# One decoder block on one core: the last column block of the output product and the layer norm behind it, rearranged

## What is computed

```
u   = x * (1 + scale) + shift
q, k, v, z_a, B, C, xc, z_b, g_a, g_b = split(u @ W_in)
...                                    # differential attention -> yA, short convolution -> yB
h   = sigmoid(g_a) * (yA @ P_a) + sigmoid(g_b) * (yB @ P_b)
out = h @ W_out
r   = 2**0.25 * x + gate * out
y   = (r - mean(r)) * rsqrt(var(r) + 1e-5) * ln_gain + ln_bias      # over the 2048 columns
```

## Time and profile before

| what | us |
|---|---|
| median of 3 runs | 1530.58 (1530.0 to 1531.59) |
| the profiled execution, its own time | 1531.4 |
| its span, first to last instruction | 1529.7 |
| PE busy in the span | 1478.7 (97%) |
| DVE busy | 860.4 (56%) |
| ACT busy | 515.6 (34%) |
| POOL busy | 67.6 (4%) |

### The profile page before, as it was taken

The page is one execution under the profiler, slowest core; times in us unless marked ns, Lnnn a source line. Parts: engine busy times, 40 slices in busy tenths (PEclk is TensorE's granted clock), DMA queues, the critical chain, the costliest instruction groups (busy, mean ns, idle before and its releaser), DMA issues.

```text
span 1529.7 us, 18414 instructions
## 1 busy us (share of the span) xinstructions
PE 1478.7 (97%) x6624; PEld 1211.3 (79%) x6624; DVE 860.4 (56%) x1182; ACT 515.6 (34%) x725; POOL 67.6 (4%) x99
## 2 busy tenths in 40 slices
PE   4999989999999999999999999999999999999993
PEld 3888867878878788887888878887888888888882
DVE  6978667658475574656756568333432323533447
ACT  2333553253432534425344253232122121411121
POOL 0000000000000000000000000100000000000004
PEclk9999999999999999999999999999999999999997
DMA  9979525352453524444254442632323232363212
GB/s 354 385 261 381 172 69 159 97 154 80 142 158 114 154 80 141 142 130 137 82 157 124 142 127 81 224 109 83 109 84 108 84 110 82 111 247 110 82 55 110
DMA packets 212359, 219.18 MB, mean 143 GB/s; under 512 B 8418, under 2 KB 160738, under 8 KB 211554
## 3 DMA queue, kind: packets, MB, share of 16 engines
q1 hardware_dynamic: 201264, 176.52, 35.3%
q0 software_dynamic: 10096, 35.66, 7.8%
q10 hardware_dynamic: 962, 6.53, 1.1%
HBM read 211.33 MB, written 7.34 MB: 143 GB/s over the span
## 4 chain that ended last, share of the span: by engine, by line
PE 95%; DVE 3%; DMA 1%; ACT 1%; issue 0%; SPq 0%; POOLq 0%; POOL 0%; ACTq 0%; DVEq 0%
PE acc L1251 29%; PE acc L1253 29%; PE acc L1252 29%; PE sc L1350 1%; PE misc L1373 1%; PE sc L1251 1%; PE sc L1253 1%; PE sc L1252 1%; DMA w_mod_in<-in_w_mod 1%; PE sc L1364 1%; DVE res L1234 1%; DVE res L1210 0%; PE sc L1300 0%; PE misc L1300 0%; PE misc L1356 0%
## 5 line engine op out<-in xcount | busy, mean ns | idle before, releaser
L1251 PE MATMUL acc<-act_hi,w_hi 128*128 128x512 f32 x1472 | 578.9, 393 | 9.9 <-ACT q_raw L503 6.1
L1253 PE MATMUL acc<-act_hi,w_lo 128*128 128x512 f32 x1472 | 574.6, 390 | 0.0
L1252 PE MATMUL acc<-act_lo,w_hi 128*128 128x512 f32 x1472 | 574.4, 390 | 0.0
L503 ACT ACTIVATE w_hi<-raw 128x1024 fp32r<-128x1024 f32 (+1 forms) x258 | 269.9, 1053 | 773.6 <-PE acc L1253 619.5
L774 DVE TENSOR_TENSOR w_lo<-raw,w_hi 128x1024 fp32r<-128x1024 f32 (+1 forms) x258 | 311.0, 1213 | 388.6 <-ACT w_hi L503 388.6
L1251 PEld LDWEIGHTS acc<-act_hi,w_hi 128*128 128x128 f32 x1472 | 277.4, 188 | 71.5 <-ACT q_raw L503 6.6
L1253 PEld LDWEIGHTS acc<-act_hi,w_lo 128*128 128x128 f32 x1472 | 277.2, 188 | 58.5
L1252 PEld LDWEIGHTS acc<-act_lo,w_hi 128*128 128x128 f32 x1472 | 277.5, 189 | 57.0 <-issue 0.2
L984 DVE SCALAR_TENSOR_TENSOR bias_acc<-bias_w,mod,bias_acc 128x512 f32<-128x512 f32 x48 | 36.1, 751 | 124.7 <-DMA bias_w<-in_w_in 124.7
L1253 PE MATMUL acc<-y_hi,w_lo 128*128 128x512 f32 x256 | 100.3, 392 | 0.0
L1252 PE MATMUL acc<-y_lo,w_hi 128*128 128x512 f32 x256 | 100.3, 392 | 0.0
(11 more groups left out here) (170 smaller groups left out, 1058.5 us busy)
## 6 DMA issues: line engine op xcount, KB each, us to landing
raw<-in_w_in SPq DMA_DIRECT2D x256, 256.0 KB
raw<-in_w_tail SPq DMA_DIRECT2D x32, 1024.0 KB
raw<-in_w_in SPq DMA_DIRECT2D x25, 1024.0 KB
w_mod_in<-in_w_mod SPq DMA_DIRECT2D x32, 512.0 KB, 8.6
w_mod_in<-in_w_mod SPq DMA_DIRECT2D x16, 1024.0 KB, 9.2
gate_in<-in_w_mod POOLq DMA_DIRECT2D x32, 512.0 KB, 4.3
bias_w<-in_w_in POOLq DMA_DIRECT2D x48, 256.0 KB, 3.3
x_in<-in_xT SPq DMA_DIRECT2D x8, 512.0 KB, 8.4
```

What stands on the lines that cost most here:

```text
L503: return act.activation(dst, src, ACT.Copy)
L1251: pe.matmul(dst, a_hi, b_hi, start=first, stop=False)
L1252: pe.matmul(dst, a_hi, b_lo, start=False, stop=False)
L1253: return pe.matmul(dst, a_lo, b_hi, start=False, stop=last)
```

## The change

In the last column block only two halves are shared by all token tiles (`SHARED` = 2). The other six are kept: four in the slots, and two in buffers of their own, `w_end_hi` and `w_end_lo`, which lie where part of `x_tok` lay. Each token tile then goes through six halves. Accordingly ACT and DVE handle halves 3, 4 and 5 of the block by the old rule and halves 6 and 7 without waiting for a slot.

The norm is made by DVE for all 2048 columns of every tile, in two instructions of 1024 columns, in the last tile in three of 1024, 640 and 384 (`Y_PARTS`). ACT makes only the square root, POOL has no part in it, `shift_col` is gone, and SP issues all stores, one for each part.

x is loaded into `res` itself, once all of h is split (`h_split` in place of `h_ready`); the product with `gate` goes into a new tile, `gated`, and L1210 reads `res` and `gated` and writes `res`.

```diff
--- before.py
+++ after.py
@@ -19,6 +19,8 @@
 
 
 from contextlib import ExitStack
+
+import itertools
 
 import numpy as np
 
@@ -57,8 +59,9 @@
 SHIFT_SLOTS = 4
 SHIFTS = D // COLS
 SCALE_STEPS = GROUPS * MOD_CHUNKS * MOD_STEPS
-V_COLS = (896, 896, 1024, 1600)
-V_FIRST = tuple(c * 5 // 8 for c in V_COLS)
+Y_PARTS = (((0, 1024), (1024, 2048)),) * (NT - 1) + (((0, 1024), (1024, 1664), (1664, 2048)),)
+Y_COUNT = tuple(itertools.accumulate(len(parts) for parts in Y_PARTS))
+SHARED = 2
 LEAD = 3
 SLOTS = 4
 
@@ -143,7 +146,7 @@
         stats = sb("stats", [P, NT, D // COLS, 6])
         mean_var = sb("mean_var", [P, NT, 2])
         rstd = sb("rstd", [P, NT])
-        shift_col = sb("shift_col", [P, NT])
+        sb("to_grid", [P, 4])
 
         raw = sb("raw", [P, 2, 4, COLS])
         w_hi = sb("w_hi", [P, SLOTS, 2, COLS], F32R)
@@ -194,7 +197,9 @@
         z_b, e_b, o_sq, rms = q_raw, q_rot, k_raw, k_rot
         h, y_hi, y_lo = stage([("h", [P, KT, T], F32), ("y_hi", [P, HEADS, T], F32R),
                                ("y_lo", [P, HEADS, T], F32R)])
-        res, x_tok = stage([("res", [P, NT, D], F32), ("x_tok", [P, NT, D], F32)])
+        res, w_end_hi, w_end_lo, gated = stage([
+            ("res", [P, NT, D], F32), ("w_end_hi", [P, 2, 2, COLS], F32R), ("w_end_lo", [P, 2, 2, COLS], F32R),
+            ("gated", [P, NT, COLS], F32)])
 
         acc = ctx.enter_context(nc.psum_tensor("acc", [P, 4, COLS], F32))
         sc = ctx.enter_context(nc.psum_tensor("sc", [P, 3, 512], F32))
@@ -282,10 +287,6 @@
         step = sem("step")
         var_ready = sem("var_ready")
         std_ready = sem("std_ready")
-        norm_ready = sem("norm_ready")
-        normed = sem("normed")
-        pool_step = sem("pool_step")
-        pool_ready = sem("pool_ready")
         y_ready = sem("y_ready")
         stored = sem("stored")
 
@@ -336,13 +337,6 @@
                 pool.wait_ge(g_stored[n], 16)
             for e in range(ENDS):
                 pool.dma_start(h[:, 4 * e:4 * e + 4, :], g_raw[:, 4 * e:4 * e + 4, :]).then_inc(g_back[e], 16)
-
-            for t in range(NT):
-                tail = res[:, t, V_COLS[t]:D]
-                pool.wait_ge(normed, t + 1)
-                pool.tensor_tensor(tail, tail, ln_g[:, V_COLS[t]:D], ALU.mult).then_inc(pool_step, 1)
-                pool.wait_ge(pool_step, t + 1)
-                pool.tensor_tensor(tail, tail, ln_b[:, V_COLS[t]:D], ALU.add).then_inc(pool_ready, 1)
 
 
         @block.sync
@@ -486,15 +480,10 @@
                 for s in range(4):
                     plain_unit(w_tail, s, i * COLS, i, 4, O0 // 2 + s)
             for t in range(NT):
-                for n in range(2):
-                    cols = slice(n * V_FIRST[t], V_COLS[t] if n else V_FIRST[t])
-                    sp.wait_ge(y_ready, 2 * t + n + 1)
-                    sp.dma_start(out[t * P:(t + 1) * P, cols], res[:, t, cols]).then_inc(stored, 16)
-                if t < NT - 1:
-                    sp.wait_ge(pool_ready, t + 1)
-                    sp.dma_start(out[t * P:(t + 1) * P, V_COLS[t]:D], res[:, t, V_COLS[t]:D]
-                                 ).then_inc(stored, 16)
-            sp.wait_ge(stored, 16 * 3 * NT)
+                for n, (c0, c1) in enumerate(Y_PARTS[t]):
+                    sp.wait_ge(y_ready, Y_COUNT[t] - len(Y_PARTS[t]) + n + 1)
+                    sp.dma_start(out[t * P:(t + 1) * P, c0:c1], res[:, t, c0:c1]).then_inc(stored, 16)
+            sp.wait_ge(stored, 16 * Y_COUNT[-1])
 
 
         @block.scalar
@@ -728,25 +717,24 @@
                 copy(act_hi[:, k, :], h[:, k, :]).then_inc(h_hi_ready, 1)
 
             act.wait_ge(half_done, O0 + BASE)
-            act.wait_ge(h_ready, KT + BASE)
-            act.dma_start(x_tok[:, :, :], x.rearrange("(t p) d -> p t d", p=P)).then_inc(late_in, 16)
+            act.wait_ge(h_split, KT)
+            act.dma_start(res[:, :, :], x.rearrange("(t p) d -> p t d", p=P)).then_inc(late_in, 16)
             act.dma_start(ln_g[:, :], ln_gain.broadcast_to([P, D])).then_inc(late_in, 16)
             act.dma_start(ln_b[:, :], ln_bias.broadcast_to([P, D])).then_inc(late_in, 16)
             with act.Fori(0, D // COLS - 1) as i:
                 for s in range(OUT_HALVES):
                     round_at(O0, i, OUT_HALVES, s + LEAD)
-            for s in range(OUT_HALVES - LEAD):
-                round_at(O0, D // COLS - 1, OUT_HALVES, s + LEAD)
+            last = D // COLS - 1
+            for s in range(LEAD, SHARED + SLOTS):
+                round_at(O0, last, OUT_HALVES, s)
+            for n in range(2):
+                f = O0 + last * OUT_HALVES + SHARED + SLOTS + n
+                act.wait_ge(raw_landed[(f // 2) % 2], 64 * (f // 4 + 1))
+                copy(w_end_hi[:, n], raw[:, (f // 2) % 2, 2 * n:2 * n + 2, :]).then_inc(hi_ready, 1)
             for t in range(NT):
                 act.wait_ge(var_ready, t + 1)
                 act.activation(rstd[:, t:t + 1], mean_var[:, t, 1:2], ACT.Sqrt, bias=eps_col[:, 0:1]
                                ).then_inc(std_ready, 1)
-                act.wait_ge(norm_ready, t + 1)
-                act.activation(res[:, t, V_COLS[t]:D], res[:, t, V_COLS[t]:D], ACT.Identity,
-                               scale=rstd[:, t:t + 1], bias=shift_col[:, t:t + 1]).then_inc(normed, 1)
-            act.wait_ge(pool_ready, NT)
-            act.dma_start(out[(NT - 1) * P:T, V_COLS[-1]:D], res[:, NT - 1, V_COLS[-1]:D]
-                          ).then_inc(stored, 16)
 
 
         @block.vector
@@ -1202,13 +1190,13 @@
                     else:
                         dve.wait_ge(half_done, i * OUT_HALVES + (O0 + OUT_HALVES + BASE))
                     dve.wait_ge(h_split, KT)
-                    dve.tensor_tensor(res[:, t, cols], acc[:, t, :], gate[:, cols], ALU.mult
+                    dve.tensor_tensor(gated[:, t, :], acc[:, t, :], gate[:, cols], ALU.mult
                                       ).then_inc(bank_drained[t], 1)
                 dve.wait_ge(late_in, 48)
                 for t in tiles:
                     dve.wait_ge(bank_drained[t], i + (O_BLOCK0 + 1 + BASE))
-                    own(dve.scalar_tensor_tensor(res[:, t, cols], x_tok[:, t, cols], ALPHA,
-                                                 res[:, t, cols], ALU.mult, ALU.add))
+                    own(dve.scalar_tensor_tensor(res[:, t, cols], res[:, t, cols], ALPHA,
+                                                 gated[:, t, :], ALU.mult, ALU.add))
                 for t in tiles:
                     dve.wait_ge(step, base + (count[0] + count[1] - (len(tiles) - 1)))
                     own(dve.bn_stats(stats[:, t, bass.ds(i, 1), :].rearrange("p a b -> p (a b)"),
@@ -1220,28 +1208,28 @@
                 residual(i, range(NT), i * OUT_STEPS)
             close(OUT_STEPS, D // COLS - 1)
             last = D // COLS - 1
-            for s in range(OUT_HALVES - LEAD):
-                lo_half(O0, last, OUT_HALVES, s + LEAD)
-
+            for s in range(LEAD, SHARED + SLOTS):
+                lo_half(O0, last, OUT_HALVES, s)
+            for n in range(2):
+                f = O0 + last * OUT_HALVES + SHARED + SLOTS + n
+                dve.wait_ge(hi_ready, f + 1)
+                dve.tensor_tensor(w_end_lo[:, n], raw[:, (f // 2) % 2, 2 * n:2 * n + 2, :],
+                                  w_end_hi[:, n].bitcast(F32), ALU.subtract).then_inc(lo_ready, 1)
 
             for t in range(NT):
                 residual(last, (t,), 0)
                 settle()
                 dve.bn_aggr(mean_var[:, t, :], stats[:, t, :, :]).then_inc(var_ready, 1)
-                for n in range(2):
-                    cols = slice(n * V_FIRST[t], V_COLS[t] if n else V_FIRST[t])
+                for c0, c1 in Y_PARTS[t]:
                     dve.wait_ge(var_ready, t + 1)
-                    own(dve.scalar_tensor_tensor(res[:, t, cols], res[:, t, cols], mean_var[:, t, 0:1],
-                                                 ln_g[:, cols], ALU.subtract, ALU.mult))
+                    own(dve.scalar_tensor_tensor(res[:, t, c0:c1], res[:, t, c0:c1], mean_var[:, t, 0:1],
+                                                 ln_g[:, c0:c1], ALU.subtract, ALU.mult))
                 dve.wait_ge(std_ready, t + 1)
                 own(dve.reciprocal(rstd[:, t:t + 1], rstd[:, t:t + 1]))
                 settle()
-                dve.tensor_scalar(shift_col[:, t:t + 1], mean_var[:, t, 0:1], rstd[:, t:t + 1], -1.0,
-                                  ALU.mult, ALU.mult).then_inc(norm_ready, 1)
-                for n in range(2):
-                    cols = slice(n * V_FIRST[t], V_COLS[t] if n else V_FIRST[t])
-                    dve.scalar_tensor_tensor(res[:, t, cols], res[:, t, cols], rstd[:, t:t + 1],
-                                             ln_b[:, cols], ALU.mult, ALU.add).then_inc(y_ready, 1)
+                for c0, c1 in Y_PARTS[t]:
+                    dve.scalar_tensor_tensor(res[:, t, c0:c1], res[:, t, c0:c1], rstd[:, t:t + 1],
```

(12 more changed lines are left out.)

## The result

| | us |
|---|---|
| changed kernel, median of 4 runs | 1517.27 (1516.63 to 1518.71) |
| kernel before, beside it | 1530.63 (1530.0 to 1531.59) |
| ratio | 0.9911, 95% interval 0.9895 to 0.9927 |
| profiled execution's span, after / before | 1515.7 / 1529.7 |
| forecast | 1521.6, range 1519.9 to 1524.0 |

The time fell by 13.4 us where 9.0 were forecast.

What follows compares the result with a forecast made beforehand. Matmuls on TensorE bound the body; the change acts on the 24.9 us tail. Last store 9.6 us earlier, 9.0 arriving, other terms 0: profiled 1531.4 becomes 1522.4, median 1521.6 after the 0.8 offset; range 1519.9 to 1524.0.

Steps and rivals of the forecast that it cites:

- (a): Last column block: a token tile takes 8.16 us of TensorE instead of 5.44; tile 3 still full at 1504.79.
- (b): Weights of halves 5, 6 and 7 ready 1.6 to 1.9 us early, cost nothing; bounds 0 and 0.9.
- (f): Loading x into `res`: ScalarE's issues and next rounding slip about 2.3 us, covered; cost 0, bounds 0 and 2.3.
- the same cover: First output block: 6 us before TensorE wants half 3, to absorb ScalarE's slip of about 2.3 us.
- (c): VectorE alone takes 7.55 us per tile, under TensorE's 8.16, so it starts tile 3 at 1504.83, 6.36 earlier.
- (d): Last tile's norm in three parts on VectorE: last store leaves at 1512.76 instead of 1522.33, 9.6 us earlier.
- The slower rival: L1210 is dear beside running stores, not through GpSimd: 12.0 us a tile on VectorE, time about 1537; chance 4%.
- both halves that the prediction took from it: VectorE and GpSimd's port pair goes to one for a whole instruction; engine ports and DMA ports do not contend.
- one instruction per tile: Kernel before: VectorE is 6.4 us behind at tile 3 because L1210 waits for GpSimd, 0.69 us becoming 2.60 and 2.21.
- (e): Final stores, all from SP: last landing at 1515.6, so 9.0 us of the 9.6 arrive; landing bounds 2.3 and 3.3.
- the queue's sum: Tile 3's stores: 0.85 us to first data, 2.56 for 1049 KB at 410 GB/s, 0.8 to landing, giving 1515.6.
- (e), its last part: End of the program: 5.1 us from landing to span end, fixed, mostly a 4.9 wait for other engines' closing.

Runs made afterwards that it cites:

- The experiment with the old order: Changed kernel with four shared halves as before the change, norm on VectorE alone: 1523.88 us, ratio 0.9955 to the kernel before.
- the order alone: Changed kernel's order and buffers, with the norm split over VectorE, ScalarE and GpSimd as before: 1524.65 us, ratio 0.9957 to the kernel before.

## Why the prediction missed, point by point

- **Body, (a), (b), (f): right.** No gap of TensorE. The rounding of halves 6 and 7 ran right behind half 5's, and their subtraction ended at 1476.24, forecast 1476.9. ScalarE's queue issued x's load at 1336.20 instead of 1334.33, and SP's next megabyte 1.9 us later, all under the same cover.
- **VectorE, (c) and (d): right.** A tile's chain by the timeline, from 1479.82 to the end of its second pass at 1487.44: 7.62, as summed. The experiment with the old order measures 7.54 from tile to tile.
- **The slower rival: refuted.** Stores run beside L1198 and the passes, and L1198 stays at 0.69: the bytes of tile 0 move from 1487.1 to 1489.6 at 377 to 475 GB/s, over tile 1's L1198 at 1488.78. The trace agrees with the Trainium skill, "SBUF — State Buffer", in "Who interferes with whom", in both halves that the prediction took from it. That the pair of ports is given away for a whole instruction fits L1210 ending 0.54 to 0.55 us behind GpSimd's instruction in every tile where the two meet before; that transfers do not slow VectorE fits the 0.69.
- **The reading of the kernel before, "one instruction per tile": incomplete.** VectorE's timeline before, tile 1 and the start of tile 2:

```profile
1493.95 0.69 DVE L1205 TENSOR_TENSOR res<-acc,gate 128x512 f32<-128x512 f32 x1
...
1498.41 2.55 DVE L1234 SCALAR_TENSOR_TENSOR res<-res,mean_var,ln_g 128x560 f32<-128x560 f32 x2
...
1502.39 0.68 DVE L1205 TENSOR_TENSOR res<-acc,gate 128x512 f32<-128x512 f32 x1
```

VectorE needed 5.44 us for tile 0, which met no GpSimd work, and 8.4 and 8.8 for tiles 1 and 2; that makes the 6.4 us that it was behind. L1210 accounts for 1.9 and 2.1 of it. The first norm pass, L1234, took 2.55 in tile 1 where tile 0 has 1.28 for the same columns, and in tile 2 some 1.2 more than free of GpSimd. So both two-input operations wait. The forecast was not touched by it, because both waits go with GpSimd. But it says more than the prediction did: sharing a tile with GpSimd cost VectorE 8.4 to 8.8 us, and all 2048 columns alone cost it 7.54.

- **Stores, (e), the landing: nearly right.** The last issue was at 1512.2, 10.1 earlier, of which 0.5 are the body's. The landing took 3.1 us where the queue's sum gave 2.84. By the formula in the Trainium skill, "DMA: Bandwidth & Descriptors", section "Anatomy of one DMA", the estimate for one transfer alone was 2.45; the page gives that formula for transfers issued by GpSimd, and this one is SP's. The last store, and the rate in slices after (0.25 us from 1510):

```profile
out<-res SPq DMA_DIRECT2D x1, 192.0 KB, 3.1
...
GB/s 0 0 0 0 0 0 115 393 442 377 459 383 379 430 399 363 387 68 0 0 0 0 0 0 0 0 0 0 0 0 0 0 0 0 0 0 0 0 0 0
```

In all but the first and the last busy slice the rate is between 363 and 459 GB/s, so the last store's bytes come behind those of the two before it: the queue. Data begins 0.8 us behind the first issue and takes 2.6 us, as summed. (410 GB/s was no maximum: the earlier trace rows have slices up to 464. As a mean it held, 403 here.) From the last byte to the landing it is 1.0 us instead of 0.8, for which no run shows a reason.

- **The step that failed, (e), its last part:** "From landing to the end of the span it is 5.1 us, fixed". Nothing in the sum said why it should be fixed. It is 0.4 us; the other 4.6 were GpSimd's closing drain, which ends 7.2 us behind GpSimd's last compute instruction and so at 1529.5, behind the landing. I had the row: a wait of 4.9 for "PEq", in the earlier trace rows. I took it for the closing of all engines, and named no engine, because the profile names the one whose semaphore came last. The instructions of the closing itself, listed by line, show at once that four engines are done by 1524.8 and that one is not. A single tiny instruction put back (4.3 us) and the last tile taken off GpSimd (5 us gained) show that this is the cause. No rival stood on the side of a gain that large, and the range's low end of 1519.9 is 0.2 below what its own terms give (1521.6 - 0.5 - 1.0 = 1520.1).
- With the term right the sum would have been 9.0 + 4.6 = 13.6, against 13.4 measured. The two profiled spans differ by 14.0, but 0.5 of that is the body's, which the change does not explain.

What each part is worth from the kernel before, in time: the norm alone 7.0 (1530.89 to 1523.88), the order alone 6.8 (1531.47 to 1524.65), both together 13.4 to 13.7. Both experiments keep the new load of x and the tile `gated`, so what these are worth is in both numbers; the traces show no cost for them. The two parts add here because they act in different places: the order sets when VectorE gets to the last tile, and the norm frees the closing (4.6) and shortens the last tile (from its start to the last store's issue 11.1 us before, 7.9 after), less 0.8 for the landing.

## What to carry to other kernels

Read the end of a span as a race between engines, not as overhead: list the closing instructions of each engine and find the one that is late. Work moved to GpSimd near the end cost twice here, by VectorE's waits for it (8.4 to 8.8 us a tile against 7.54 alone) and by 7.2 us of drain behind its last instruction; the second is free where GpSimd's last instruction ends over 7.2 us before the last store lands. And when a slower consumer follows a producer tile by tile, spacing the tiles a little wider than the consumer's time (8.16 against 7.54 us) puts only one tile's work behind the producer's end.

## What was not expected of the hardware

The DRAIN that closes GpSimd's part of the program is long behind everything that it followed here: 7.4 us from its start for an addition of 128x4 of 0.19 us, 7.1 to 7.2 behind the end of the last compute instruction in six executions (128x4, 128x448 and 128x1024), and 13.6 to 13.8 us when what it follows is the issue of three transfers from GpSimd's queue, as at 985.2. SP's takes 7 ns, ScalarE's 0.15 to 0.8 us. The drains of TensorE and VectorE last only as long as the engine still has work: before, TensorE's ends at 1504.9 with the last matmul (1504.79), and VectorE's at 1521.3 with its last pass (1521.32). GpSimd's alone goes on for 7.2 us. What GpSimd does in that time, and whether a different last instruction would shorten it, was not tried and stays open. The two runs with a tiny addition put in a semaphore wait and an addition together; a wait alone was not tried either. That the drain's end keeps to the end of the addition, whether that takes 0.19, 1.55 or 2.67 us, speaks for the addition.
